# 16 unused bytes behind each block of 128 columns of the split weights

## The reference

```python
h = rmsnorm(x, norm1_g)
z = h @ w_in                      # 1024 x 6912: RWKV, attention and gate columns
y_a = rwkv7_time_mix(...) @ w_proj_a      # 1024 x 1024
y_b = window_sink_attention(...) @ w_proj_b
x = x + (g_a * y_a + g_b * y_b) @ w_out   # 1024 x 1024
h = rmsnorm(x, norm2_g)
u = h @ w_up                      # 1024 x 5632
c = conv_b + sum(conv_w[i] * shifted(u, i))
x = x + (silu(c_gate) * c_val) @ w_down   # 2816 x 1024
return rmsnorm(x, normf_g)
```

## Time and profile before

| what | value |
|---|---|
| the two runs | 1037.27 us, 1037.18 us |
| span of the profiled execution | 1035.3 us |
| TensorE busy | 1023.1 us, 99% |
| VectorE, ScalarE, GpSimd busy | 743.2, 518.1, 218.8 us |
| share of the chain that ended last that is TensorE | 95% |
| mean granted clock | 0.999 |

### The profile page before, as it was taken

How to read it: one execution, slowest core, us unless ns; L and a number is a source line. 1 busy time by engine, 2 the same in 40 slices (tenths; PEclk the granted TensorE clock), 3 DMA queues, 4 the chain that set the end, 5 groups by cost and what they waited for, 6 DMA issues and landing times.

```text
span 1035.3 us, 17866 instructions
## 1 busy us (share of the span) xinstructions
PE 1023.1 (99%) x6666; PEld 825.4 (80%) x6666; DVE 743.2 (72%) x1233; ACT 518.1 (50%) x869; POOL 218.8 (21%) x290
## 2 busy tenths in 40 slices
PE   8999999999999999999999999999999999999997
PEld 6888888778777777777877888888888888888886
DVE  5334667788988878788777466357777777789786
ACT  6435766844535445344544332365445544457744
POOL 8542346220221312303220444200000000000000
PEclk9999999999999999999999999999999999999999
DMA  7874465430303313123335876713323333336663
GB/s 204 234 219 143 132 223 179 101 82 25 82 25 72 85 62 86 44 73 90 117 97 161 252 235 219 248 40 103 101 87 96 101 101 87 95 117 215 205 190 117
DMA packets 161287, 133.20 MB, mean 129 GB/s; under 512 B 32729, under 2 KB 137735, under 8 KB 161223
## 3 DMA queue, kind: packets, MB, share of 16 engines
q1 hardware_dynamic: 147552, 88.37, 29.3%
q0 software_dynamic: 13520, 43.90, 13.8%
q10 hardware_dynamic: 151, 0.04, 0.0%
HBM read 111.83 MB, written 20.45 MB: 128 GB/s over the span
## 4 chain that ended last, share of the span: by engine, by line
PE 95%; DVE 1%; ACT 1%; issue 1%; DMA 1%; POOL 0%; ACTq 0%; DVEq 0%; POOLq 0%
PE ps L2070 14%; PE ps L2073 14%; PE ps L2072 14%; PE ps L2026 6%; PE ps L2028 5%; PE ps L2027 5%; PE ps L2611 3%; PE ps L2612 3%; PE ps L2613 3%; PE ps L2242 3%; PE ps L2372 2%; PE ps L2393 2%; PE ps L2183 2%; PE ps L2545 1%; PE ps L2546 1%; PE ps L2547 1%
## 5 line engine op out<-in xcount | busy, mean ns | idle before, releaser
L1340 DVE TENSOR_TENSOR wlo<-raw,whi 128x1024 fp32r<-128x1024 f32 x106 | 142.2, 1341 | 126.5 <-ACT whi L874 108.6
L874 ACT ACTIVATE whi<-raw 128x1024 fp32r<-128x1024 f32 x116 | 122.8, 1059 | 128.9 <-PE ps L2073 117.2
L2070 PE MATMUL ps<-xnh,whi 128*128 128x512 f32 x336 | 130.7, 389 | 0.0
L2072 PE MATMUL ps<-xnl,whi 128*128 128x512 f32 x336 | 130.7, 389 | 0.0
L2073 PE MATMUL ps<-xnh,wlo 128*128 128x512 f32 x336 | 130.7, 389 | 0.0
L2070 PE MATMUL ps<-xh,whi 128*128 128x512 f32 x232 | 91.5, 394 | 1.0 <-DVE xl L1358 1.0
L2072 PE MATMUL ps<-xl,whi 128*128 128x512 f32 x232 | 90.4, 390 | 0.0
L2073 PE MATMUL ps<-xh,wlo 128*128 128x512 f32 x232 | 90.3, 389 | 0.0
L2026 PE MATMUL ps<-xh,whi 128*128 128x512 f32 x192 | 88.6, 462 | 0.0
L2028 PE MATMUL ps<-xh,wlo 128*128 128x512 f32 x192 | 76.0, 396 | 0.0
L2027 PE MATMUL ps<-xl,whi 128*128 128x512 f32 x192 | 75.2, 392 | 0.0
(11 more groups left out here) (424 smaller groups left out, 2483.0 us busy)
## 6 DMA issues: line engine op xcount, KB each, us to landing
raw<-in_w_in SPq DMA_DIRECT2D x108, 256.0 KB, 3.3
raw<-in_w_up SPq DMA_DIRECT2D x88, 256.0 KB, 3.0
wrow<-in_w_down POOLq DMA_DIRECT2D x22, 512.0 KB, 4.8
raw<-weight_scratch SPq DMA_DIRECT2D x44, 256.0 KB, 3.5
raw<-in_w_down SPq DMA_DIRECT2D x32, 256.0 KB, 2.9
weight_scratch<-wrow POOLq DMA_DIRECT2D x11, 512.0 KB, 3.4
gates_scratch<-gst POOLq DMA_DIRECT2D x16, 256.0 KB, 3.2
raw<-in_w_proj_b SPq DMA_DIRECT2D x16, 256.0 KB, 4.1
```

What stands on the lines that cost most here:

```text
L874: act.activation(flat(whi[:, hb]), flat(raw[:, b]), ACT.Copy).then_inc(w_hi, 1)
L1340: dve.tensor_tensor(flat(lo[:, hb]), flat(raw[:, b]), flat(hi[:, hb]).bitcast(F32), ALU.subtract).then_inc(w_lo, 1)
L2070: pe.matmul(ps[bank][:, :], whi[:, hb, k, :], hi(k), start=first and k == 0, stop=False)
L2072: pe.matmul(ps[bank][:, :], whi[:, hb, k, :], lo(k), start=False, stop=False)
```

## The change

Each block of 128 columns of `whi` and `wlo` is given a row of 132 numbers, 528 bytes, of which the first 128 are used. 528 is 2 x 256 + 16, so block k of the first half has place 16k (0 to 112) and block k of the second half 128 + 16k (128 to 240). The splits of ScalarE and VectorE write and read eight runs of 128 numbers in place of one of 1024, and the streamed operand of the products with `w_out` and `w_down` is four runs of 128 in place of one of 512. `whi` and `wlo` become 256 bytes longer each, the arena ends 512 bytes earlier, and `raw` moves by these 512 bytes to another address of place 0. No instruction is added, taken out or moved on any engine or queue, and `whx`, `wlx`, `who` and `wlo2` lie as before.

```diff
+ROW = P + 4
...
-        weight_bytes = (RAW + 2 * HL) * KT * P * 4
+        weight_bytes = (RAW * P + 2 * HL * ROW) * KT * 4
...
-        whi = sb("whi", [P, HL, KT, P], F32R)
-        wlo = sb("wlo", [P, HL, KT, P], F32R)
+        whi = sb("whi", [P, HL, KT, ROW], F32R)[:, :, :, 0:P]
+        wlo = sb("wlo", [P, HL, KT, ROW], F32R)[:, :, :, 0:P]
...
-                act.activation(flat(whi[:, hb]), flat(raw[:, b]), ACT.Copy).then_inc(w_hi, 1)
+                act.activation(whi[:, hb], raw[:, b], ACT.Copy).then_inc(w_hi, 1)
...
-                dve.tensor_tensor(flat(lo[:, hb]), flat(raw[:, b]), flat(hi[:, hb]).bitcast(F32),
+                dve.tensor_tensor(lo[:, hb], raw[:, b], hi[:, hb].bitcast(F32),
                                   ALU.subtract).then_inc(w_lo, 1)
...
                 hi, lo = (who, wlo2) if k >= KT - 2 else (whi, wlo)
-                hi, lo = flat(hi[:, k % 2]), flat(lo[:, k % 2])
-                o, cols, toks = ps[2 * j + half][:, :], slice(half * T, (half + 1) * T), \
+                hi, lo = hi[:, k % 2], lo[:, k % 2]
+                o, cols, toks = ps[2 * j + half][:, :], slice(half * NT, (half + 1) * NT), \
                     slice(j * P, (j + 1) * P)
                 pe.matmul(o, mh[:, k, toks], hi[:, cols], start=start, stop=False)
```

More of the change, by code:

```diff
@@ L880, in split_down @@
                 act.wait_ge(slot_done, N_DOWN if t < 4 else n - 3)
-                act.activation(flat(dst[:, t % 2, 0:kn]), flat(raw[:, n % RAW, 0:kn]), ACT.Copy)\
+                act.activation(dst[:, t % 2, 0:kn], raw[:, n % RAW, 0:kn], ACT.Copy)\
                     .then_inc(w_hi, 1)
@@ L1216, in split_out @@
                     act.wait_ge(slot_done, done)
-                act.activation(flat(dst[:, n % 2]), flat(raw[:, b]), ACT.Copy).then_inc(w_hi, 1)
+                act.activation(dst[:, n % 2], raw[:, b], ACT.Copy).then_inc(w_hi, 1)
             def normed(m):
@@ L1549, in weights_half @@
                     dve.wait_ge(w_hi, n + 1)
-                last = dve.tensor_tensor(flat(wlo[:, n % HL, ks]), flat(raw[:, slot(n), ks]),
-                                         flat(whi[:, n % HL, ks]).bitcast(F32), ALU.subtract)
+                last = dve.tensor_tensor(wlo[:, n % HL, ks], raw[:, slot(n), ks],
+                                         whi[:, n % HL, ks].bitcast(F32), ALU.subtract)
                 last.then_inc((w_half, w_lo)[half], 1)
@@ L1833, in split_down @@
                 dve.wait_ge(w_hi, n + 1)
-                dve.tensor_tensor(flat(lo[:, t % 2, 0:kn]), flat(raw[:, n % RAW, 0:kn]),
-                                  flat(hi[:, t % 2, 0:kn]).bitcast(F32), ALU.subtract)\
+                dve.tensor_tensor(lo[:, t % 2, 0:kn], raw[:, n % RAW, 0:kn],
+                                  hi[:, t % 2, 0:kn].bitcast(F32), ALU.subtract)\
                     .then_inc(w_lo, 1)
@@ L2607, in down @@
                 hi, lo = ((whi, wlo), (whx, wlx))[t % 4 // 2]
-                hi, lo = flat(hi[:, t % 2]), flat(lo[:, t % 2])
-                o, cols = ps[bank + half][:, :], slice(wcol * T, (wcol + 1) * T)
+                hi, lo = hi[:, t % 2], lo[:, t % 2]
+                o, cols = ps[bank + half][:, :], slice(wcol * NT, (wcol + 1) * NT)
                 h_hi, h_lo = (part[:, half * P:(half + 1) * P] for part in h)
```

## The result

The changed kernel takes 1050.97 us (1050.78 and 1051.16) against 1037.22 before: a ratio of 1.0133, with a 95% interval from 1.0104 to 1.0163. It is 13.75 us slower. The spans are 1048.9 and 1035.3 us, so nearly all of it, 13.6 us, lies inside the profiled program.

What follows compares the result with a forecast made beforehand. The prediction took TensorE, busy for 99%, as the bound. Held blocks 0, streamed blocks 0 and hidden splits 0 left the time at 1037.2 us, bounds 1034.3 to 1046.5, with a range of 1033 to 1050 us.

Steps and rivals of the forecast that it cites:

- What bounds the kernel, and how many products are touched: TensorE, busy 99% of the span, bounds the kernel; the change touches 2943 products, 2565 held blocks move.
- Holding a block from another place: Products holding moved `whi` or `wlo` blocks on TensorE: taken as 0, bounds -1 to +3 ns each.
- The upper end: Bound of +3 ns on each of 2943 TensorE products with moved blocks, +8.8 us in all.
- Streaming four blocks in place of one run: 378 products streaming `whi` or `wlo` in `w_out` and `w_down`: breaks taken as 0, under 0.5 us.
- The splits: ScalarE and VectorE splits in eight runs: some 2 ns more in 1226, hidden by 3.1 us of cover per tile.
- Rival 1: Held and streamed operands at place 0 collide; spreading saves 11.0 ns a product, 32.4 us, giving 1004.8 us; chance 0.04.
- Rival 2: Odd multiples of 16 read slower on TensorE: loads 278 ns, 70 us, streaming 40 us, together 1147 us; chance 0.07.
- The range: Whole-kernel time expected 8 times in 10 between 1033 and 1050 us.
- The chances by sign at 2%: Whole-kernel time, with 2% as threshold: faster 0.04, same 0.89, slower 0.07.
- the slower case under 2%: Cost beyond the forecast bounds but under 2%, say 3 to 7 ns a product; chance 0.06.

Runs made afterwards that it cites:

- m4_history: TensorE alone: two place pairs (0 with 0, 16 with 0) after 16 predecessors, then the changed kernel's block order: 226.7; 226.7 or 233.3; 232.1 ns between starts.
- e6_rows28: Kernel before, with streamed activations of `w_in`, `w_proj_a` and `w_up` at place 28, the rest as before: 1039.9 us, ratio 1.0025.
- e1_gaps: Kernel before, with `whi` and `wlo` in one another's gaps: separate runs, every block still at place 0: 1037.33 us, ratio 0.9999.
- e2_weights128: Kernel before, `whi` and `wlo` unbroken but all blocks at place 128, activations at 0: 1052.88 us, ratio 1.0149.
- m1_table: TensorE alone: 256 groups of 14 float32r products, 16 held by 16 streamed places; 388 to 400 ns, 226.6 to 236.7 between starts.
- e3_all128: Kernel before, with everything from the arena on moved to place 128, held and streamed operands alike: 1037.41 us, ratio 1.0003.
- e4_weights16: Kernel before, `whi` and `wlo` unbroken but all blocks at place 16, activations at 0: 1042.93 to 1052.79 us, ratio 1.0117.
- m3_reads: TensorE alone: six kinds of product over the places, with fewer held columns or operands read from one word; one-word row 381 ns, 218.7 between starts.

## Why the prediction was wrong

**What bounds the kernel, and how many products are touched:** right. The loss came through the distance between products and no wait was added; 2943 products had been counted, and it is the part of them outside the heads that pays.

**The step that failed is "Holding a block from another place", the term taken as 0 with bounds of -1 and +3 ns.** It measured +5.3 ns in `w_up` by the stage's time, +5.4 by the distance between starts in its steady part (232.1 against 226.7) and +5.2 in the records' mean (394.2 against 389). The bounds came from the gate and lora products, chosen because their operands lie at 32 and 224. They are single triples between float16 products. What costs is a rhythm that a long stream settles into, and these rows belong to the one stage that lost nothing (-0.1 us). They were also compared by duration, on the ground that a nanosecond of distance would show as a nanosecond of duration. That holds only roughly: 387.4 and 389 stand for the same 226.7 ns (m4_history), 395 and 397 for the same 233.3, and 389.4 stood for 228.6 (e6_rows28), so a bound of -1 ns from a row of 388 was no bound on the cost. Their neighbours with every operand at place 0 had 393 and 397 there against 389 in the dense stages: that difference said that 389 isn't the cost of a product but of a product in an undisturbed stream, and I read it as the spread of float16 neighbours and went on to use 389 as if it were the reference for both. (The stream of before shows it too: after one pause in `w_down` its durations went 393, 393, 397, 389, 395, 393 before 389 came back.) The upper end should have been taken from the earlier trace rows, +4 to +8 ns, which gives 12 to 24 us.

**"Streaming four blocks in place of one run", taken as 0:** the runs are free, as e1_gaps shows with its 389 on line 2546. But the place of a streamed block costs as that of a held one does, 5 to 7 ns in the medians of lines 2546 and 2612 and 7.9 ns for each of the 144 touched products of `w_out` by the stage's 1.1 us. This term counted the breaks and not the places, and the 378 products had only the held blocks' bounds.

**The splits, taken as hidden:** right in both ways. They take as long as before, and there was cover. (The rows of `e` were called no multiple of 16 "either"; the change's blocks all start at a multiple of 16, which alters nothing here.)

**Rival 1** had the right picture, two reads in each other's way and a surplus of 13 ns that has to come from somewhere, and the wrong sign. 381 ns with a row of one word shows that 8 ns of the surplus are a matter of reading; but equal places are the best case where the row lies at an even multiple of 16, not the worst. **Rival 2**, with a weight load that grows, did not occur: the loads stayed at 188 ns, and with the row at 0 the odd multiples of 16 are no worse than the even ones.

**The range** ended at 1050 and the time was 1050.97. The chances by sign at 2% hold, since 1.3% is inside, but the slower case under 2% had been given 0.06, when no row excluded it.

**The rules of the Trainium skill.** The Trainium skill's page "SBUF — State Buffer" (Specifications (TRN2)) gives lines of 16 bytes and a penalty for crossing into a new one. That a block at a multiple of 16 costs nothing was the prediction's conclusion from it, and for TensorE e2_weights128 and m1_table contradict that conclusion: 389 against 395 ns with the same number of lines of 16 bytes. The N / 2.4 + 2.5 of the Trainium skill's page "TensorE: Matmul & The Clock Gate" (Back-to-back issue gap), 215.8 ns for 512 columns, isn't reached by any of the float32r products here; the nearest is the row of one word, 218.7 ns between starts.

## What to carry to other kernels

When a stream of products is the bound, look whether its duration is one constant or several: one constant is a rhythm that a layout holds, and a price read from isolated products says nothing of it. Take the price itself from the distance between starts. For float32r products of 512 columns, keep the operand that TensorE holds and the one that it streams at the same address modulo 256, at an even multiple of 16 (0 and 128 were tried in the kernel), and let a pad or a new tensor ahead of them be a multiple of 256 bytes. Test a layout in a long stream by itself before it goes into the kernel, after more than one predecessor and in the kernel's own order.

## What the runs showed of the hardware

- A float32r product of 512 columns that holds 128 columns costs 226.7 to 236.7 ns between starts, depending on the addresses of its two operands modulo 256 (m1_table); the weight load's duration does not show it (188 to 189 ns in the dense stages).
- The value goes by the difference of the two places: moving both by 32 leaves most pairs as they were (m1_table), and moving both by 128 left the kernel's time (e3_all128). With the row at an even multiple of 16 the differences 0, 16 and 240 gave 226.7 ns; with the row at an odd multiple equal places gave 230.0 in seven of eight cases (m1_table).
- For one pair there can be two stable cycles, 226.7 or 233.3 ns between starts with 16 and 0, and what ran before chooses (m4_history). With such a layout a kernel's time varied from run to run, 1042.9 to 1052.8 us in e4_weights16; that each run's stages had fallen into one cycle or the other is inferred from its one trace.
- After a block at another place, or after a pause, a stream can need up to ten products to come back to its constant (up to eight in m4_history, up to ten on `whx` in the changed kernel, seven after the pause in `w_down` of the kernel before).
- The recorded duration and the distance between starts can part by 1 to 2 ns: 387.4 and 389 for 226.7, 395 and 397 for 233.3.
- With the row read from a single word, the product takes 381 ns at every place, 218.7 between starts (m3_reads).
- What sets the cycles, and why the rows at 28 cost 228.6 ns between starts in e6_rows28 and 226.7 alone, stays open.
